# Cache attention, last sequence: the high parts of the output weights on GpSimd instead of ScalarE

## The chip, the cores and the metric

The kernel runs on one core of a Trainium2 chip. The metric is the device time of one execution in microseconds (us), the median of several runs. A profiled execution also has a span, from the first to the last instruction that the trace shows.

The core's engines run beside each other, each through its own list of instructions in order, and wait for each other by semaphores: TensorE (PE in the rows, PEld for its weight loads), VectorE (DVE), ScalarE (ACT), GpSimd (POOL) and SyncE (SP), which here issues most DMAs.

## The reference

One layer of a decoder runs for a prompt of 1024 tokens and for 8 decode tokens, each of which attends to its own 8192 cached positions. What matters here is the decode attention, in which a key is an up-projected latent beside a rotary part, normalised together, and the output projection that follows it:

```python
def update(carry, ckv_blk, kpe_blk, mask):
    m, l, acc = carry
    k = mla_keys(ckv_blk, kpe_blk, w_uk, g_kn).astype(jnp.float32)
    s = jnp.einsum('bqhd,bkhd->bhqk', qf, k) * scale
    ...
mixed = jnp.concatenate([rms_norm(pool_out, g_out[:POOL_WIDTH]),
                         rms_norm(attn_out, g_out[POOL_WIDTH:])], axis=-1)
x = x + mixed @ lp['w_o']
```

The gains `g_out` belong to rows of `w_o`, so the kernel multiplies them into the weights. All is 32-bit. A matmul operand is held as a high part, rounded to the type that TensorE takes in one pass (`fp32r` in the rows), and a low part, the rest; a product is then three matmuls: high by high, high by low, low by high.

## The kernel before, in words

The work goes through stages: inputs and heads, prompt attention, the cache stage with the output projection (`cache_and_merge`), gate and up projection, down projection. The change lies in the cache stage, in the last of its 8 sequences.

**The loop.** A sequence's 8192 positions are 64 tiles of 128, taken in 32 pairs; the loop variable is `n` (on GpSimd also `u`). Every engine has its own loop over the same pairs, written out by hand, and the order in each list is the order of the work:

- TensorE: `turn` (L1734) transposes the latents of pair n + 1 into `TT`; `keys` (L1760) waits for the residual `lo` of pair n (`lo_done`) and makes the keys of its two tiles, six matmuls each (L1768). At n = 18 `weigh` (L1772) sums the latents of the sequence before, weighted by the probabilities.
- ScalarE: `hi` (L1919) rounds the transposed latents; `squares` (L2011) squares the keys of pair n - 1 (L2016) and copies their scores (L2017), tile by tile.
- VectorE: `lo` (L2101) is the residual; `sums` (L2216) adds the squares of pair n - 1, first tile (L2220); then work of single values of n; then `rotary_scores` (L2223) reduces GpSimd's product of pair n - 2 (L2225); then `sums` for the second tile; at every fourth n `rotary_sums` (L2228).
- GpSimd: `product` (L1626, instruction at L1634) multiplies the rotary keys of pair n by the query, into one of two buffers. It waits until VectorE has reduced the product of pair n - 2 (`product_read`).

**The score tail.** When a sequence is through, GpSimd turns raw scores into normalised ones: `tail_mean` (L1639), `tail_raw` (L1650), `tail_norm` (L1658, a Newton step of four instructions, L119 to L122), `tail_scale` (L1664). Most instructions wait for the one before by a semaphore (`step`). In the last sequence three quarters of this (48 tiles, 384 numbers in a partition) are done inside the loop, after the products of n = 25, 26, 28 and 29; the rest follows the loop.

**The output weights.** While the last sequence runs, `w_o` (8 blocks of 128 rows, two halves of 512 columns, j = 0 to 15) is loaded and split. SyncE loads half j into one of two buffers `w_raw` when the low part of half j - 2 is made (L1567). ScalarE multiplies by the gain column and rounds: the high part `w_o_hi` (`split_w_o`, L1943, instruction at L1949). VectorE makes the low part `w_o_lo` (`split_w_o`, L2131, instruction at L2135). Halves 0 to 11 are made in the loop, one at each n of

```python
HALF_AT = tuple(n for n in range(19, PAIRS) if n != 28)
```

on ScalarE after the squares, on VectorE between the two `sums`, ahead of `rotary_scores`. At n = 28 VectorE makes the residual of the first mixed tile instead (L2143), of which ScalarE makes the square and the high part at n = 25 and 26. Halves 12 to 15 follow the loop. Then `project` (L1814) multiplies the mixed rows of 9 tiles by the weights.

Of the kernel before, what the change touches and what calls it, by code (L numbers as in the profile page):

```python
# [12 lines left out]
ALU = mybir.AluOpType  # L13
# [8 lines left out]
NB = 8  # L22
# [1354 lines left out]
HALF_AT = tuple(n for n in range(19, PAIRS) if n != 28)  # L1377
# [23 lines left out]
def cache_and_merge(nc, io, keep):  # L1401

    START, PACE = 36, 7
    with ExitStack() as stack:
# [97 lines left out]
        dve_step = c.sem("dve_step")  # L1502

        w_o_in = [c.sem(f"w_o_in{n}") for n in range(2)]
        w_o_hi_done, w_o_lo_done = c.sem("w_o_hi_done"), c.sem("w_o_lo_done")
        m_in = [c.sem(f"m_in{n}") for n in range(3)]
        x_in = [c.sem(f"x_in{n}") for n in range(XS)]
        stored = [c.sem(f"stored{n}") for n in range(XS)]
# [103 lines left out]
        @block.gpsimd  # L1612
        def _(pool):
            def chunk_sums(i):

                n = width(i)
                pool.wait_ge(mix_squared, i + 1)
                step(nc.gpsimd.tensor_tensor(msq[:, :, 0:2, 0:n], msq[:, :, 0:2, 0:n], msq[:, :, 2:4, 0:n], ALU.add))
                nc.gpsimd.tensor_tensor(msq[:, :, 0, 0:n], msq[:, :, 0, 0:n], msq[:, :, 1, 0:n], ALU.add)\
                  .then_inc(chunks_added, 1)  # L1620

            step = Steps(pool, pool_step)

            def product(b, u):

                par, k, made = b % 2, 2 * (u % 4), b * PAIRS + u  # L1626
                if u == 0:
                    pool.wait_ge(q_in[par], 16 * (b // 2 + 1))
                if u % 4 == 0:
                    pool.wait_ge(slot_in[par * CHUNKS + u // 4], 32 * (b // 2 + 1))  # L1630
                if made >= 2:
                    pool.wait_ge(product_read, made - 1)
                keys = kpe[:, (b * CHUNKS + u // 4) % RING, k * DR:(k + 2) * DR].rearrange("p (k d) -> p k d", d=DR)
                nc.gpsimd.tensor_tensor(products[u % 2][:].rearrange("p (k h) d -> p k h d", h=NH),  # L1634
                                        keys.unsqueeze(2).to_broadcast([P, 2, NH, DR]),
                                        q_row[par].rearrange("p (h d) -> p h d", d=DR).unsqueeze(1)
                                        .to_broadcast([P, 2, NH, DR]), ALU.mult).then_inc(product_made, 1)

            def tail_mean(b, a=0, z=TILES):  # L1639

                mean = ss[:, b % 2, a:z]
                if b >= 1 and a == 0:
                    pool.wait_ge(shifted, b)
                pool.wait_ge(summed, b * TILES + z)
                pool.wait_ge(pe_summed, b * CHUNKS + z // 8)
                step(nc.gpsimd.tensor_tensor(mean, mean, kss[:, b % 2, a:z].unsqueeze(2)
                                             .to_broadcast([P, z - a, NH]), ALU.add))
                nc.gpsimd.tensor_scalar(mean, mean, 1.0 / DH, EPS, ALU.mult, ALU.add).then_inc(averaged, 1)

            def tail_raw(b, a=0, z=TILES):  # L1650

                pool.wait_ge(scored, b * TILES + z)
                step(nc.gpsimd.tensor_tensor(raw[:, b % 2, a:z], raw[:, b % 2, a:z],
                                             keep.coef[:, b, :].unsqueeze(1).to_broadcast([P, z - a, NH]), ALU.mult))
                pool.wait_ge(product_read, b * PAIRS + z // 2)
                step(nc.gpsimd.tensor_tensor(raw[:, b % 2, a:z], raw[:, b % 2, a:z], rot[:, b % 2, a:z], ALU.add))

            def tail_norm(b, part=0, a=0, z=TILES):  # L1658

                pool.wait_ge(averaged, b + 1 + part)  # L1660
                pool.wait_ge(guessed, b + 1 + part)
                step(newton_rsqrt(nc.gpsimd, step, guess[:, a:z], ss[:, b % 2, a:z], guess[:, a:z], tmp[:, a:z]))

            def tail_scale(b, a=0, z=TILES):  # L1664
                step(nc.gpsimd.tensor_tensor(raw[:, b % 2, a:z], raw[:, b % 2, a:z], guess[:, a:z], ALU.mult))

            def tail_own(b):
                nc.gpsimd.tensor_copy(raw[:, b % 2, TILES, :], keep.s_new[:, b, :]).then_inc(complete, 1)

            def tail_shift(b):  # L1670
                pool.wait_ge(reduced, b + 1)
                nc.gpsimd.tensor_tensor(raw[:, b % 2], raw[:, b % 2], top_all[:].unsqueeze(1)
                                        .to_broadcast([P, TILES + 1, NH]), ALU.subtract).then_inc(shifted, 1)

            def paced(b, n):
                pool.wait_ge(summed, (b - 1) * TILES + START + PACE * n // 2)
                gather(nc, io, keep, b, (n,))

            def sequence(par, b, r):
                for n in range(PAIRS):  # L1680
                    if b == 0 and n % 4 == 0 and 4 <= n < 4 * (CHUNKS - 2):
                        pool.wait_ge(summed, 2 * n)
                        gather(nc, io, keep, 0, (n // 4 + 2,))
                    product(b, n)
                    if b >= 1:
                        if n == MEAN_AT:
                            tail_mean(b - 1)
                        if n == RAW_AT:
                            tail_raw(b - 1)
                        if n == NORM_AT:  # L1690
                            tail_norm(b - 1)
                        if n == OWN_AT:
                            tail_scale(b - 1)
                            tail_own(b - 1)
                        if n == SHIFT_AT:
                            tail_shift(b - 1)
                    if b + 1 < NB and n in GATHER_AT:
                        if GATHER_AT[n][0] == 0:
                            if b == 0:
                                pool.wait_ge(keep.mixed_stored, 16 * (1 + NH // 2))  # L1700
                            else:
                                pool.wait_ge(weighted, b)
                        for k in GATHER_AT[n]:
                            paced(b + 1, k)
                    if b == NB - 1 and n == 25:
                        tail_mean(b, *PARTS[0])
                    if b == NB - 1 and n == 26:
                        tail_raw(b, *PARTS[0])
                    if b == NB - 1 and n == 28:
                        tail_norm(b, 0, *PARTS[0])  # L1710
                    if b == NB - 1 and n == 29:
                        tail_scale(b, *PARTS[0])

            gather(nc, io, keep, 0, (1, 2))
            sequences(pool, sequence)
            chunk_sums(0)
            b = NB - 1
            tail_mean(b, *PARTS[1])
            tail_raw(b, *PARTS[1])
            tail_norm(b, 1, *PARTS[1])  # L1720
            tail_scale(b, *PARTS[1])
            tail_own(b)
            chunk_sums(1)
            tail_shift(b)
            for i in range(2, NT):
                chunk_sums(i)
            down.gpsimd(pool)
# [184 lines left out]
        def _(act):  # L1912
            def sequence(par, b, r):
                later = b > 0
                for n in range(PAIRS):
# [16 lines left out]
                        square_rotary(par, b, n // 4)  # L1932
                    if b < NB - 1 and n in HI_AT:
                        split_w(b + 1, HI_AT.index(n))
                    if b == NB - 1:
                        if n in HALF_AT:
                            split_w_o(HALF_AT.index(n))
                        if n == 25:
                            square_mixed(0)
                        if n == 26:  # L1940
                            split_mixed(0)

            def split_w_o(j):  # L1943

                k, g = divmod(j, 2)
                act.wait_ge(w_o_in[g], 16 * (k + 1))
                if j == 0:
                    act.wait_ge(weighted, NB - 1)
                nc.scalar.activation(w_o_hi[:, k, g * 512:(g + 1) * 512], w_raw[g][:], ACT.Copy,  # L1949
                                     scale=keep.g_out[:, k:k + 1]).then_inc(w_o_hi_done, 1)  # L1950

            def square_mixed(i):

# [115 lines left out]
        def _(dve):  # L2069
# [61 lines left out]
            def split_w_o(j):  # L2131

                k, g = divmod(j, 2)
                dve.wait_ge(w_o_hi_done, j + 1)
                nc.vector.scalar_tensor_tensor(out=w_o_lo[:, k, g * 512:(g + 1) * 512], in0=w_raw[g][:],  # L2135
                                               scalar=keep.g_out[:, k:k + 1],
                                               in1=w_o_hi[:, k, g * 512:(g + 1) * 512].bitcast(F32), op0=ALU.mult,
                                               op1=ALU.subtract).then_inc(w_o_lo_done, 1)
# [736 lines left out]
```

## Time and profile before

| | us |
|---|---|
| median of 3 runs | 2211.56 |
| the runs | 2207.08, 2211.56, 2211.88 |
| the profiled execution | 2210.82 |
| its span | 2209.0 |
| TensorE busy | 2155.2 |
| VectorE busy | 1530.3 |
| ScalarE busy | 972.2 |
| GpSimd busy | 702.2 |

How to read it: "busy" adds up the instructions of an engine, whether or not something waits for them. The loop over the cache runs from about 415 to 1303 us of the span, the last of its 8 sequences at the end; the granted TensorE clock is full in all slices of the page. A row of the timeline gives start, duration, engine, line, operation, what is written from what, shapes, and in brackets how long the engine had been idle before and who released it.

### The profile page before, as it was taken

The page shows a single profiled execution, that of the slowest core. Times are in us where ns is not written, and L with a number is a line of the kernel's source. Part 1 is how long each engine was busy: PE and PEld are TensorE (multiplying, and loading weights), DVE is VectorE, ACT ScalarE, POOL GpSimd, SP SyncE. Part 2 cuts the span into 40 slices and gives each one's busy share as a digit, 9 for nine tenths or more (in the row PEclk, how much of TensorE's full clock was granted, in tenths as well). Part 3 has the DMA queues.
Part 4 walks back from the last instruction along what each step waited for, and adds up shares of the span by engine and source line. Part 5 has one row for each costly group of instructions (what it writes and reads, how often), then busy time and mean ns, then how long its engine had stood idle before and what let it go on. Part 6 is the DMA issues. An engine that isn't in the chain of part 4 may idle for free.

```text
span 2209.0 us, 33857 instructions
## 1 busy us (share of the span) xinstructions
PE 2155.2 (98%) x12537; PEld 1801.5 (82%) x12537; DVE 1530.3 (69%) x2353; ACT 972.2 (44%) x2273; POOL 702.2 (32%) x765
## 2 busy tenths in 40 slices
PE   8998899999999999999999989999999999999999
PEld 7987566788787878787878767799999999977776
DVE  4447676688787878787878785666767677654345
ACT  4445566556565656565656553312111111233333
POOL 1554211367474747474747352100000000000000
PEclk9999999999999999999999999999999999999999
DMA  5210100243131313131314032221111111044353
GB/s 163 66 29 1 61 16 20 84 141 124 66 115 59 121 53 128 48 132 46 134 43 149 25 129 96 78 75 44 47 47 47 47 47 44 23 174 148 132 188 125
DMA packets 95811, 183.20 MB, mean 83 GB/s; under 512 B 9416, under 2 KB 65568, under 8 KB 87311
## 3 DMA queue, kind: packets, MB, share of 16 engines
q1 hardware_dynamic: 79933, 96.53, 13.3%
q0 software_dynamic: 15744, 84.93, 11.3%
q8 instruction: 79, 1.29, 0.2%
q14 instruction: 55, 0.45, 0.1%
HBM read 167.39 MB, written 14.36 MB: 82 GB/s over the span
## 4 chain that ended last, share of the span: by engine, by line
PE 77%; DVE 3%; ACT 0%; issue 0%; DMA 0%; POOL 0%; SPq 0%; ACTq 0%; DVEq 0%; POOLq 0%
PE ca_banks L1768 31%; PE ca_banks L2376 22%; PE ca_banks L2649 11%; PE ca_banks L1744 5%; PE ca_banks L1828 4%; PE ca_banks L1780 3%; PE ca_banks L2625 0%; DVE ca_cells L2225 0%; DVE ca_cells L2220 0%; DVE ca_lo L2101 0%; PE ca_banks L1859 0%; DVE ca_room L2487 0%; DVE ca_down_lo L2689 0%; DMA ca_x<-in_x_prompt 0%; ACT ca_down_hi L2680 0%
## 5 line engine op out<-in xcount | busy, mean ns | idle before, releaser
L2016 ACT ACTIVATE ca_banks<-ca_banks 128x512 f32<-128x512 f32 x512 | 298.2, 582 | 324.1 <-PE ca_banks L1768 319.6
L1768 PE MATMUL ca_banks<-cache_w_hi,ca_hi 128*128 128x512 f32 x1024 | 427.6, 418 | 6.5 <-DVE ca_lo L2101 5.6
L2220 DVE TENSOR_REDUCE ca_cells<-ca_banks 128x8 f32<-128x512 f32 x512 | 352.3, 688 | 87.9 <-ACT ca_banks L2016 72.7
L1768 PE MATMUL ca_banks<-cache_w_lo,ca_hi 128*128 128x512 f32 x1024 | 403.0, 394 | 0.0
L1768 PE MATMUL ca_banks<-cache_w_hi,ca_lo 128*128 128x512 f32 x1024 | 401.3, 392 | 0.0
L1768 PEld LDWEIGHTS ca_banks<-cache_w_hi,ca_lo 128*128 128x128 f32 x1024 | 193.1, 189 | 46.5
L1768 PEld LDWEIGHTS ca_banks<-cache_w_hi,ca_hi 128*128 128x128 f32 x1024 | 192.9, 188 | 44.7 <-DVE ca_lo L2101 10.4
L1768 PEld LDWEIGHTS ca_banks<-cache_w_lo,ca_hi 128*128 128x128 f32 x1024 | 193.6, 189 | 32.3
L1634 POOL TENSOR_TENSOR ca_product<-cache_kpe,attn_q_row_odd 128x512 f32<-128x512 f32 x128 | 164.7, 1290 | 171.4 <-DVE ca_cells L2225 169.9
L2101 DVE TENSOR_TENSOR ca_lo<-ca_banks,ca_hi 128x512 fp32r<-128x512 f32 x256 | 175.0, 684 | 56.7 <-ACT ca_hi L1919 56.2
L1634 POOL TENSOR_TENSOR ca_product<-cache_kpe,ca_q_row_even 128x512 f32<-128x512 f32 x128 | 164.7, 1293 | 130.6 <-DVE ca_cells L2225 129.3
L1919 ACT ACTIVATE ca_hi<-ca_banks 128x512 fp32r<-128x512 f32 x256 | 154.5, 604 | 55.7 <-PE ca_banks L1744 55.7
L2225 DVE TENSOR_REDUCE ca_cells<-ca_product 128x16 f32<-128x512 f32 x256 | 172.9, 676 | 2.9 <-POOL ca_product L1634 2.9
L2572 POOL DMA_DIRECT2D out_new_conv_prompt<-ca_y x1 | 0.6, 612 | 542.3 <-ACT ca_y L2663 542.3
L2487 DVE RECIPROCAL ca_room<-ca_room 128x1032 f32<-128x1032 f32 x22 | 145.3, 6603 | 0.8
L2689 DVE TENSOR_TENSOR ca_down_lo<-ca_down_raw,ca_down_hi 128x1024 fp32r<-128x1024 f32 x44 | 53.9, 1225 | 97.0 <-ACT ca_down_hi L2680 97.0
L2421 ACT ACTIVATE ca_room<-ca_banks 128x1032 f32<-128x1032 f32 x22 | 22.8, 1036 | 219.9 <-PE ca_banks L2376 219.9
L2649 PE MATMUL ca_banks<-ca_down_hi,ca_g_hi 128*128 128x512 f32 x352 | 113.9, 405 | 2.2 <-DVE ca_gT L2490 1.9
L2376 PE MATMUL ca_banks<-mlp_h_hi,ca_gate_hi 128*128 128x344 f32 x528 | 113.4, 321 | 0.6 <-DVE mlp_h_lo L2185 0.6
L2376 PE MATMUL ca_banks<-mlp_h_lo,ca_gate_hi 128*128 128x344 f32 x528 | 113.3, 320 | 0.0
L2376 PE MATMUL ca_banks<-mlp_h_hi,ca_gate_lo 128*128 128x344 f32 x528 | 112.7, 319 | 0.0
L2376 PE MATMUL ca_banks<-mlp_h_hi,ca_up_hi 128*128 128x344 f32 x528 | 112.2, 321 | 0.0
(400 smaller groups left out, 4323.3 us busy)
## 6 DMA issues: line engine op xcount, KB each, us to landing
ca_down_raw<-in_w_down SPq DMA_DIRECT2D x44, 512.0 KB, 3.3
keep_w_uv<-in_w_gate SPq DMA_DIRECT2D x22, 512.0 KB, 3.8
ca_up_raw<-in_w_up SPq DMA_DIRECT2D x22, 512.0 KB, 3.6
keep_ctx<-in_w_down SPq DMA_DIRECT2D x22, 512.0 KB, 3.7
late_room<-in_x_prompt SPq DMA_DIRECT2D x8, 512.0 KB, 3.6
ca_m<-mixed_scratch SPq DMA_DIRECT2D x8, 512.0 KB, 5.3
ca_w_raw<-in_w_o SPq DMA_DIRECT2D x16, 256.0 KB, 2.5
ca_x<-in_x_prompt SPq DMA_DIRECT2D x8, 512.0 KB
```

Source lines behind the costliest of these rows:

```text
L1634: nc.gpsimd.tensor_tensor(products[u % 2][:].rearrange("p (k h) d -> p k h d", h=NH), keys.unsqueeze(2).to_broadcast([P, 2, NH, DR]), q_ro ...
L1744: last = nc.tensor.transpose(TT[:, n % 2, (2 * t + ck) * P:(2 * t + ck + 1) * P], src, keep.ident[:])
L1768: last = nc.tensor.matmul(KK[:, t, :], x[:, n % 2, t, ck, :], w[:, par, ck, :], start=(m == 0), stop=(m == 5))
L1828: last = nc.tensor.matmul(OUT[0:n, a, g, :], h[:, k, 0:n], w[:, k, g * 512:(g + 1) * 512], start=(k == 4 * a and q == 0), stop=(k == 4 * a ...
L1919: nc.scalar.activation(hi[:, n % 2], TT[:, n % 2, :].rearrange("p (t c k) -> p t c k", t=2, c=2), ACT.Copy).then_inc(hi_done, 1)
L2016: nc.scalar.activation(SQ[:, t, :], KK[:, t, :], ACT.Square).then_inc(squared, 1)
L2101: nc.vector.tensor_tensor(lo[:, n % 2], TT[:, n % 2, :].rearrange("p (t c k) -> p t c k", t=2, c=2), hi[:, n % 2].bitcast(F32), ALU.subtra ...
L2220: nc.vector.tensor_reduce(ss[:, par, 2 * n + t, :], SQ[:, t, :].rearrange("p (h d) -> p h d", d=DN), AX.X, ALU.add).then_inc(summed, 1)
L2225: nc.vector.tensor_reduce(rot[:, par, 2 * u:2 * u + 2, :].rearrange("p t h -> p (t h)"), products[u % 2][:], AX.X, ALU.add).then_inc(produ ...
L2376: ins = nc.tensor.matmul(GU[kind][:, j, :], w[kind][:, k, :], h[:, k, j * F3:(j + 1) * F3], start=(k == 0 and n == 0), stop=(k == DC - 1 a ...
L2487: link(nc.vector.reciprocal(sig, sig))
L2649: last = nc.tensor.matmul(self.OUT[t][:, h, :], g[b][:, t * P:(t + 1) * P], w[b][:, h * 512:(h + 1) * 512], start=(f == 0 and k == 0), sto ...
```

## The change

GpSimd gets a function `raise_w_o`, called in the last sequence at each n of `HALF_AT`, ahead of `product(b, n)`. It makes the high part of halves 0 to 11 by one `tensor_scalar` with the gain column; at the first it also waits for `weighted`, as ScalarE did. ScalarE's `split_w_o` is no longer called in the loop; it makes halves 12 to 15 after it, as before, and counts them by a semaphore of their own. VectorE waits for the one count or the other.

```diff
-        w_o_hi_done, w_o_lo_done = c.sem("w_o_hi_done"), c.sem("w_o_lo_done")
+        w_o_hi_done, w_o_hi_rest, w_o_lo_done = c.sem("w_o_hi_done"), c.sem("w_o_hi_rest"), c.sem("w_o_lo_done")
...
+            def raise_w_o(j):
+
+                k, g = divmod(j, 2)
+                pool.wait_ge(w_o_in[g], 16 * (k + 1))
+                if j == 0:
+                    pool.wait_ge(weighted, NB - 1)
+                nc.gpsimd.tensor_scalar(w_o_hi[:, k, g * 512:(g + 1) * 512], w_raw[g][:], keep.g_out[:, k:k + 1], None,
+                                        ALU.mult).then_inc(w_o_hi_done, 1)
...
+                    if b == NB - 1 and n in HALF_AT:
+                        raise_w_o(HALF_AT.index(n))
                     product(b, n)
...
-                    if b == NB - 1:
-                        if n in HALF_AT:
-                            split_w_o(HALF_AT.index(n))
-                        if n == 25:
-                            square_mixed(0)
-                        if n == 26:
-                            split_mixed(0)
+                    if b == NB - 1 and n == 25:
+                        square_mixed(0)
+                    if b == NB - 1 and n == 26:
+                        split_mixed(0)
...
                 act.wait_ge(w_o_in[g], 16 * (k + 1))
-                if j == 0:
-                    act.wait_ge(weighted, NB - 1)
                 nc.scalar.activation(w_o_hi[:, k, g * 512:(g + 1) * 512], w_raw[g][:], ACT.Copy,
-                                     scale=keep.g_out[:, k:k + 1]).then_inc(w_o_hi_done, 1)
+                                     scale=keep.g_out[:, k:k + 1]).then_inc(w_o_hi_rest, 1)
...
-                dve.wait_ge(w_o_hi_done, j + 1)
+                dve.wait_ge(w_o_hi_done, min(j + 1, len(HALF_AT)))
+                if j >= len(HALF_AT):
+                    dve.wait_ge(w_o_hi_rest, j + 1 - len(HALF_AT))
```

## Rows read from the trace of the kernel before

**Rows 1.** The page, busy time, share of the span and instructions of each engine.
```profile
PE 2155.2 (98%) x12537; PEld 1801.5 (82%) x12537; DVE 1530.3 (69%) x2353; ACT 972.2 (44%) x2273; POOL 702.2 (32%) x765
```
**Rows 2.** The chain that ended last, in order of time: start, duration, work.
```profile
1213.32 2.78 PE ca_banks L1768 x12
1216.54 2.78 PE ca_banks L1768 x12
...
1245.62 7.44 PE ca_banks L1780 x130
...
1281.90 3.06 PE ca_banks L1768 x12
...
1300.69 3.03 PE ca_banks L1768 x12
```
**Rows 3.** The timeline, slots 25 and 26 of the last sequence.
```profile
1278.00 0.58 ACT L2016 ACTIVATE ca_banks<-ca_banks 128x512 f32<-128x512 f32 x1 [0.69 <-PE ca_banks L1768]
...
1278.55 0.72 ACT L1949 ACTIVATE ca_w_o_hi<-ca_w_raw,keep_g_out 128x512 fp32r<-128x512 f32 x1
...
1279.31 0.75 DVE L2135 SCALAR_TENSOR_TENSOR ca_w_o_lo<-ca_w_raw,keep_g_out,ca_w_o_hi 128x512 fp32r<-128x512 f32 x1 [0.50 <-ACT ca_w_o_hi L1949]
...
1279.98 0.68 DVE L2225 TENSOR_REDUCE ca_cells<-ca_product 128x16 f32<-128x512 f32 x1
...
1280.57 0.68 DVE L2220 TENSOR_REDUCE ca_cells<-ca_banks 128x8 f32<-128x512 f32 x1
...
1280.73 1.27 POOL L1634 TENSOR_TENSOR ca_product<-cache_kpe,attn_q_row_odd 128x512 f32<-128x512 f32 x1 [2.28 <-DVE ca_cells L2225]
...
1281.17 0.68 DVE L2101 TENSOR_TENSOR ca_lo<-ca_banks,ca_hi 128x512 fp32r<-128x512 f32 x1
...
1281.90 0.50 PE L1768 MATMUL ca_banks<-cache_w_hi,ca_hi 128*128 128x512 f32 x1 [0.18 <-DVE ca_lo L2101]
```
**Rows 4.** Line L1949, ScalarE's high parts: durations (ns min/median/max), who waited for them.
```profile
L1949 ACT ACTIVATE ca_w_o_hi<-ca_w_raw,keep_g_out x16: 722/724/726, 1257.0 to 1311.1; 128x512 fp32r<-128x512 f32 x16
...
  DVE ca_w_o_lo L2135: 8.0, 14
```
**Rows 5.** The timeline again, slots 19, 27, 28, 30 and 31.
```profile
1257.76 0.75 DVE L2135 SCALAR_TENSOR_TENSOR ca_w_o_lo<-ca_w_raw,keep_g_out,ca_w_o_hi 128x512 fp32r<-128x512 f32 x1 [1.39 <-ACT ca_w_o_hi L1949]
...
1286.31 0.75 DVE L2135 SCALAR_TENSOR_TENSOR ca_w_o_lo<-ca_w_raw,keep_g_out,ca_w_o_hi 128x512 fp32r<-128x512 f32 x1 [0.51 <-ACT ca_w_o_hi L1949]
...
1290.83 0.68 DVE L2225 TENSOR_REDUCE ca_cells<-ca_product 128x16 f32<-128x512 f32 x1
...
1291.65 1.28 POOL L1634 TENSOR_TENSOR ca_product<-cache_kpe,attn_q_row_odd 128x512 f32<-128x512 f32 x1 [2.36 <-DVE ca_cells L2225]
...
1297.00 1.29 POOL L1634 TENSOR_TENSOR ca_product<-cache_kpe,attn_q_row_odd 128x512 f32<-128x512 f32 x1
1297.12 1.73 DVE L2135 SCALAR_TENSOR_TENSOR ca_w_o_lo<-ca_w_raw,keep_g_out,ca_w_o_hi 128x512 fp32r<-128x512 f32 x1 [0.37 <-ACT ca_w_o_hi L1949]
...
1301.45 0.75 DVE L2135 SCALAR_TENSOR_TENSOR ca_w_o_lo<-ca_w_raw,keep_g_out,ca_w_o_hi 128x512 fp32r<-128x512 f32 x1 [0.21 <-ACT ca_w_o_hi L1949]
```
**Rows 6.** Groups of GpSimd by line and shape: busy us, mean ns, idle before.
```profile
L1634 POOL TENSOR_TENSOR ca_product<-cache_kpe,attn_q_row_odd 128x512 f32<-128x512 f32 x128 | 164.7, 1290 | 171.4 <-DVE ca_cells L2225 169.9
...
L121 POOL TENSOR_SCALAR keep_w_uv<-keep_w_uv 128x512 f32<-128x512 f32 x7 | 4.3, 620 | 0.6
...
L1653 POOL TENSOR_TENSOR ca_cells<-ca_cells,attn_coef 128x384 f32<-128x384 f32 x1 | 1.0, 1015 | 0.0
...
L1646 POOL TENSOR_TENSOR ca_cells<-ca_cells 128x384 f32<-128x384 f32 x1 | 0.9, 862 | 0.0
...
L121 POOL TENSOR_SCALAR keep_w_uv<-keep_w_uv 128x384 f32<-128x384 f32 x1 | 0.5, 512 | 0.1
...
L1130 POOL TENSOR_SCALAR keep_ctx<-keep_ctx 8x8 f32<-8x8 f32 x1 | 0.2, 239 | 0.1
...
L1134 POOL TENSOR_SCALAR keep_ctx<-keep_ctx 8x8 f32<-8x8 f32 x1 | 0.2, 186 | 0.1
```

## Prediction

> **What bounds the kernel now.** I read the page first, then the chain of waits, then the timeline of the stretch that the diff touches. The page says that TensorE is busy for nearly the whole span, while ScalarE and GpSimd have room [rows 1]; by that alone, work moved between these two costs nothing. The averages hide the stretch that matters. In the chain, a pair of cache tiles (one turn n of the loop, below "slot n") normally follows the one before after 1216.54 - 1213.32 = 3.22 us: TensorE's own twelve products and four transposes [rows 2]. In slots 19 to 31 of the last sequence the pace is slower: from slot 26 (1281.90) to slot 31 (1300.69) there are five slots in 18.79 us, 3.76 each, and the row at 1281.90 is released by VectorE, not by TensorE's own queue [rows 2, 3]. So this stretch, some 45 us long, is bound by a ring of other engines, and the change rebuilds that ring.
>
> **The ring now** [rows 3]. ScalarE squares the second tile (1278.00), then makes the high half (1278.55 to 1279.27); VectorE, idle for 0.50, starts the low half at 1279.31, then the rotary reduction 0.67 later, then one sum, then the residual `ca_lo` at 1281.17, and TensorE starts at 1281.90. The high half, 0.72 each, delayed VectorE by 8.0 us in 14 of the 16 halves [rows 4]. GpSimd is not in the ring: its product starts at 1280.73, just after the reduction that frees its buffer, and is needed two slots later.
>
> **Taken away.** Twelve ScalarE instructions, 12 x 0.72 = 8.7 us busy, and with them VectorE's waits. Worth at most: the whole stretch back at TensorE's pace. The low halves of slots 19 and 31 start at 1257.76 and 1301.45, 43.69 us apart [rows 5]; twelve slots at 3.22 are 38.64, so 5.0 us is the ceiling of the gain.
>
> **Put in: a wait, and what queues behind it.** GpSimd runs in order. In slot n it now does the high half, then `product(n)`, then (slots 25, 26, 28, 29) pieces of the score tail. `product(n)` waits for rotary reduction n-2, which VectorE does in slot n *behind* its low half, and the low half waits for GpSimd's high half, which stands behind `product(n-1)`. That closes a new ring of one slot: low half, reduction, product, next high half, next low half. Its length from rows:
> - low half to reduction 1279.98 - 1279.31 = 0.67; reduction 0.68; hand-over to GpSimd 0.07 (1280.66 to 1280.73) in one slot and 0.14 (1291.51 to 1291.65) in another, mean 0.10 [rows 3, 5];
> - product 1.29 [rows 6]; high half on GpSimd, r, unknown; hand-over to VectorE about 0.05 (1279.27 to 1279.31 from ScalarE) [rows 3].
>
> Together 2.79, taken as 2.80 + r, per slot.
>
> **The price r.** No row has GpSimd scale by a per-partition column into this type, so I bound it. Below: a GpSimd tensor_scalar of the same 128x512 with constants, 0.62. Above: the two-input form, 1.29 [rows 6]. One input, one output and the same element count put it next to 0.62; I add 0.05, the difference of the one-operation and the two-operation form at 8x8 (0.239 and 0.186) [rows 6], since this one has one operation: **r = 0.67**. The ring is then 3.47 a slot: above TensorE's 3.22, below the 3.64 of today (43.69 / 12). Plain slots get slightly faster.
>
> The Trainium skill (GPSIMD Engine Reference, section 4.1 Engine selection) sends elementwise work to VectorE, calling GpSimd about 2x slower with two inputs and near line rate with one. By the 2x and VectorE's 0.75 low half r would be 1.5 and the change 15 us slower, an estimate; the one-input row of this trace, 0.62, sides with the page's second half.
>
> **The tail pieces.** Today they delay only a product that nobody needs for two slots. Now each stands between a product and the next high half, so in the ring in full. With 0.86 and 1.02 for the two kinds of 128x384 two-input operation, 0.51 for the one-input one, and 0.09 (0.6 / 7) after each for its step wait [rows 6]: mean, slot 25, 0.86 + 0.09 + 0.51 = 1.46; raw, slot 26, 2 x 1.11 = 2.22; scale, slot 29, 1.11: together 4.79. Slot 28 has no half: from the low half of slot 27 (1286.31) VectorE runs without a wait to the reduction of slot 28 (1290.83), 4.52 [rows 5]; plus 0.68, 0.10 and 1.29 is 6.59; the norm piece, four operations, is 0.86 + 1.02 + 0.51 + 1.02 + 4 x 0.09 = 3.77; then r and 0.05. From slot 27 to slot 29 that is 10.41 + r.
>
> **The sum.** In slot 19 VectorE was ready 1.39 before it started: 1257.76 - 1.39 = 1256.37 [rows 5]. GpSimd's first half waits only for the weighted sum, over at 1245.62 + 7.44 = 1253.06 [rows 2], so it is in time. From there ten plain slots (19 to 27, 29 to 31), the three tail pieces and the double slot: 10 x (2.80 + r) + 4.79 + 10.41 + r = 43.20 + 11r. The low half of slot 31 starts at 1299.57 + 11r = 1306.94, against 1301.45: **5.5 us later**. The residual that TensorE waits for stands behind the low half on VectorE, so TensorE is late by the same. With r = 0.62 the loss is 4.9, with r = 1.29 it is 12.3; the change breaks even only at r = 0.17.
>
> **The rest costs nothing.** The loads of the next halves on SyncE wait for low halves two back; a ring of over 3.4 us a slot leaves over 6 us for them. The four last halves stay on ScalarE, and they, the remaining loads, GpSimd's last tail quarter and the projection all follow slot 31, so they shift with it; nothing later waits for something that isn't shifted. ScalarE's lighter queue gives nothing more, since the ring no longer passes it.
>
> **The shared port.** In slot 30 a low half took 1.73 instead of 0.75, started while a GpSimd product (1297.00, 1.29 long) was running [rows 5]. The new ring keeps low halves and GpSimd apart, since each waits for the other, so I charge nothing.
> The Trainium skill (SBUF — State Buffer, Who interferes with whom) says that a VectorE instruction with two SBUF inputs and a GpSimd one that reads SBUF block each other for a whole instruction; the 1.73 agrees, and the sum would be the same by it.
>
> **Rivals.**
> *A. The new ring does not bind, and the change is faster.* One mechanism: GpSimd runs the half while VectorE is busy with sums and residual, and every slot returns to 3.22. It decides below r = 3.22 - 2.80 = 0.42, with the tail pieces hidden besides. Gain 5.0: 2205.8. Against it: the cheapest row is 0.62 [rows 6], and the order in the code leaves no place to hide a tail piece. Chance 0.04.
> *B. An even swap.* Today's pace is already 3.64, the new ring 3.47; if GpSimd's hand-overs and step gaps are shorter than I charge, or the tail pieces partly hide, little is left of the loss. With all three pieces of slots 25, 26 and 29 free it is 5.5 - 4.8 = +0.7, 2211.5; halfway, 2214. For it: the forecast lies near the line. Against it: each piece is in program order ahead of a half that VectorE awaits. Chance 0.24, and 0.02 that ScalarE stays in the ring by another way (its squares and copies), with no change to see.
> *C. GpSimd pays the two-input price*, for the column operand or the rounding to the matmul type: r up to 1.29, +12.3, 2223.1. The Trainium skill (GPSIMD Engine Reference, section 4.1) points this way only for two inputs. For it: no row of the exact form. Against it: the one-input rows. Chance 0.18.
>
> **The numbers.** Forecast, chance 0.52: the profiled execution took 2210.82 (span 2209.0), 0.7 below the median of the runs, 2211.56. 2210.82 + 5.5 = 2216.3; its own range, r from 0.62 to 0.85, is 2215.7 to 2218.3. The range over cases goes from B's end, 2211.0, to C's, 2223.2. About 0.2%, 4.4 us, is what a measurement of this kernel can tell from no change: slower by more is the forecast and C, 0.70; within is B, 0.26; faster is A, 0.04.
>
> **What would show it.** Right: GpSimd's new line at 0.62 to 0.85 a half; VectorE's idle time before the low halves released by GpSimd, about 0.4 in plain slots and 1.5 to 4 us in slots 26, 27, 29 and 30; GpSimd's idle time before its products still ended by the reduction; low halves about 3.47 apart in slots 19 to 25; slot 31's low half some 50.6 us after slot 19's readiness. Wrong: TensorE at 3.22 a slot there (A), low halves over 4 us apart in plain slots (C), or no long wait in slots 26, 27, 29 and 30 (B).

## The result and the profile after

The changed kernel took 2226.46 us in the median of 6 runs against 2208.01 for the kernel before in runs beside them: a ratio of 1.0076, 95% interval 1.0061 to 1.0090, or 13.5 to 19.9 us slower. The direction was forecast; the size, 5.5 us within 2211.0 to 2223.2, was not.

The profiled execution took 2221.05, the shortest of the six, and entered the stretch of the change 2.9 us earlier than the one before did. So the traces are compared over that stretch alone, from the start of the weighted sum in slot 18 (first product of that line) to the first product with the output weights. The first fence is the busy time in the stretch before (start and end, length, then busy us and instructions of TensorE, its weight loads, VectorE, ScalarE and GpSimd, the granted clock, the DMA share, GB/s), the second the same after.

```profile
1245.62:1304.41 58.79, 54.63 (x350) 40.32 (x351) 46.02 (x75) 36.59 (x91) 27.50 (x24) 1.00 0.16 54
```
```profile
1242.69:1315.91 73.22, 58.80 (x351) 43.16 (x351) 45.00 (x75) 29.78 (x79) 44.25 (x36) 0.93 0.13 44
```

The stretch is 73.22 - 58.79 = 14.4 us longer: this is where the time went. After it the two traces take the same to within 1.2 us (2209.0 - 1304.41 = 904.6 and 2219.3 - 1315.91 = 903.4). ScalarE is 6.8 us lighter; GpSimd is 16.8 us heavier. On the page of the changed kernel (busy time, then the chain that ended last) the averages hardly move [rows 1], but GpSimd has entered the chain:

```profile
PE 2157.3 (97%) x12537; PEld 1800.9 (81%) x12537; DVE 1528.7 (69%) x2353; ACT 964.7 (43%) x2261; POOL 719.1 (32%) x777
...
PE 76%; DVE 2%; POOL 2%; issue 1%; DMA 0%; ACT 0%; SPq 0%; POOLq 0%; DVEq 0%; ACTq 0%
```

The chain of waits of the changed kernel, in order of time, shows the new ring turn by turn; one turn, slot 20 to 21 (start, duration, work):

```profile
1259.15 1.28 POOL ca_product L1634
1260.43 1.56 POOL ca_w_o_hi L1645
1261.99 0.03 issue
1262.02 0.04 DVE ca_w_o_lo L2143
1262.05 0.63 issue
1262.68 0.69 DVE ca_cells L2233
1263.37 0.07 issue
1263.45 1.27 POOL ca_product L1634
```

Product, high half, low half (its successor starts 0.67 after it), reduction, product: 4.30 us, and TensorE, whose 3.22 filled the chain before [rows 2], is not in it. The groups of GpSimd's new line (shapes, count, busy us, mean ns) and the waits in the stretch (who waited for whom: us, times, longest):

```profile
L1645 POOL TENSOR_SCALAR ca_w_o_hi<-ca_w_raw,keep_g_out 128x512 fp32r<-128x512 f32 x12 | 18.8, 1567 | 5.9 <-PE ca_banks L1791 5.5
```
```profile
DVE ca_w_o_lo L2143 <- POOL ca_w_o_hi L1645: 20.2, 11, 4.9
...
PE ca_banks L1779 <- DVE ca_lo L2107: 12.8, 8, 4.6
```

A high half takes 1.57 us on GpSimd, not 0.67, and VectorE waits 20.2 us for GpSimd. In the kernel before it waited 4.7 us for ScalarE in the stretch; the 8.0 us of [rows 4] count the four halves behind the loop too.

```profile
DVE ca_w_o_lo L2135 <- ACT ca_w_o_hi L1949: 4.7, 12, 1.4
```

The timeline has the low halves of slots 19, 23 to 27 and 29 to 31 (the tail pieces come in at 26, 27, 29 and 30), and TensorE behind that of slot 29:

```profile
1253.36 0.74 DVE L2143 SCALAR_TENSOR_TENSOR ca_w_o_lo<-ca_w_raw,keep_g_out,ca_w_o_hi 128x512 fp32r<-128x512 f32 x1
...
1270.56 0.75 DVE L2143 SCALAR_TENSOR_TENSOR ca_w_o_lo<-ca_w_raw,keep_g_out,ca_w_o_hi 128x512 fp32r<-128x512 f32 x1 [1.12 <-POOL ca_w_o_hi L1645]
...
1274.84 0.75 DVE L2143 SCALAR_TENSOR_TENSOR ca_w_o_lo<-ca_w_raw,keep_g_out,ca_w_o_hi 128x512 fp32r<-128x512 f32 x1 [0.81 <-POOL ca_w_o_hi L1645]
...
1279.18 0.75 DVE L2143 SCALAR_TENSOR_TENSOR ca_w_o_lo<-ca_w_raw,keep_g_out,ca_w_o_hi 128x512 fp32r<-128x512 f32 x1 [1.20 <-POOL ca_w_o_hi L1645]
...
1284.99 0.75 DVE L2143 SCALAR_TENSOR_TENSOR ca_w_o_lo<-ca_w_raw,keep_g_out,ca_w_o_hi 128x512 fp32r<-128x512 f32 x1 [2.67 <-POOL ca_w_o_hi L1645]
...
1291.43 0.75 DVE L2143 SCALAR_TENSOR_TENSOR ca_w_o_lo<-ca_w_raw,keep_g_out,ca_w_o_hi 128x512 fp32r<-128x512 f32 x1 [3.30 <-POOL ca_w_o_hi L1645]
...
1303.31 0.75 DVE L2143 SCALAR_TENSOR_TENSOR ca_w_o_lo<-ca_w_raw,keep_g_out,ca_w_o_hi 128x512 fp32r<-128x512 f32 x1 [4.89 <-POOL ca_w_o_hi L1645]
...
1305.90 0.79 PE L1779 MATMUL ca_banks<-cache_w_hi,ca_hi 128*128 128x512 f32 x1 [4.57 <-DVE ca_lo L2107]
...
1308.66 0.75 DVE L2143 SCALAR_TENSOR_TENSOR ca_w_o_lo<-ca_w_raw,keep_g_out,ca_w_o_hi 128x512 fp32r<-128x512 f32 x1 [2.21 <-POOL ca_w_o_hi L1645]
...
1312.94 0.75 DVE L2143 SCALAR_TENSOR_TENSOR ca_w_o_lo<-ca_w_raw,keep_g_out,ca_w_o_hi 128x512 fp32r<-128x512 f32 x1 [1.14 <-POOL ca_w_o_hi L1645]
```

### The profile page after: what moved, and what is told of

It is laid out like the page before. It is cut to its first block, busy times and chain, and to the rows that moved or that the text cites. A ratio compares the mean times of both kernels' runs of the same rounds, so it can differ in the third digit from the quotient of the medians.

```text
span 2219.3 us, 33861 instructions
## 1 busy us (share of the span) xinstructions
PE 2157.3 (97%) x12537; PEld 1800.9 (81%) x12537; DVE 1528.7 (69%) x2353; ACT 964.7 (43%) x2261; POOL 719.1 (32%) x777
## 3 DMA queue, kind: packets, MB, share of 16 engines
q8 instruction: 79, 1.29, 0.2%
## 4 chain that ended last, share of the span: by engine, by line
PE 76%; DVE 2%; POOL 2%; issue 1%; DMA 0%; ACT 0%; SPq 0%; POOLq 0%; DVEq 0%; ACTq 0%
PE ca_banks L1779 30%; PE ca_banks L2384 22%; PE ca_banks L2657 11%; PE ca_banks L1755 5%; PE ca_banks L1839 4%; PE ca_banks L1791 3%; POOL ca_w_o_hi L1645 1%; POOL ca_product L1634 1%; DVE ca_cells L2233 1%; PE ca_banks L2633 0%; DVE ca_cells L2228 0%; PE ca_banks L1870 0%; DVE ca_room L2495 0%; DMA ca_x<-in_x_prompt 0%; DVE ca_lo L2107 0%
## 5 line engine op out<-in xcount | busy, mean ns | idle before, releaser
L1779 PEld LDWEIGHTS ca_banks<-cache_w_hi,ca_hi 128*128 128x128 f32 x1024 | 194.1, 190 | 54.4 <-DVE ca_lo L2107 20.2
```

Source lines behind the costliest of these rows:

```text
L1779: last = nc.tensor.matmul(KK[:, t, :], x[:, n % 2, t, ck, :], w[:, par, ck, :], start=(m == 0), stop=(m == 5))
```

## The experiments

All are edits of the changed kernel. The two kernels that mix forms were run once, for their rows. "Stretch" is the one above: 58.79 us in the kernel before, 73.22 in the changed one, each read from the one trace of its kernel. A ratio is to the kernel before in runs beside that experiment, with its 95% interval. Two questions: why is the high half so dear, and is its place in the ring the whole loss?

**Six forms in one kernel.** Each half takes one of six forms in turn.

```diff
-                nc.gpsimd.tensor_scalar(w_o_hi[:, k, g * 512:(g + 1) * 512], w_raw[g][:], keep.g_out[:, k:k + 1], None,
-                                        ALU.mult).then_inc(w_o_hi_done, 1)
+                hi, raw, col, form = w_o_hi[:, k, g * 512:(g + 1) * 512], w_raw[g][:], keep.g_out[:, k:k + 1], j % 6
+                if form == 0:
+                    made = nc.gpsimd.tensor_scalar(hi, raw, col, None, ALU.mult)
+                elif form == 1:
+                    made = nc.gpsimd.tensor_scalar(hi, raw, col, 1.0, ALU.mult, ALU.mult)
+                elif form == 2:
+                    made = nc.gpsimd.tensor_scalar(hi, raw, 1.0, None, ALU.mult)
+                elif form == 3:
+                    made = nc.gpsimd.tensor_scalar(hi, raw, 1.0, 1.0, ALU.mult, ALU.mult)
+                elif form == 4:
+                    made = nc.gpsimd.tensor_tensor(hi, raw, col.to_broadcast([P, 512]), ALU.mult)
+                else:
+                    made = nc.gpsimd.tensor_copy(hi, raw)
+                made.then_inc(w_o_hi_done, 1)
```

> The twelve halves on GpSimd are made by six forms in turn (j modulo 6): column and no second operation, column and a second operation by 1.0, constant 1.0 and no second operation, two constants, a two-input product with the column broadcast, and a plain copy. Where a constant or a copy stands, the gain is left out of the high part (the low part, made from the gained weights less the high part, takes it up). Theory 'one operation is the slow form': halves without a second operation take about 1.56, with one about 0.62 to 0.7, whether column or constant. Rival 'the column operand': 1.56 wherever the column stands as an operand (forms 0 and 1), 0.62 for constants. Rival 'rounding to the matmul type': all of them at 1.3 or more. In each, if the ring of one slot sets the pace, the low halves are 2.72 plus that half's price apart (4.28 measured less 1.56); if something else sets it, the distance does not follow the price.

GpSimd's groups by line, in the order of forms 0, 2, 4, 1, 3, 5:

```profile
L1647 POOL TENSOR_SCALAR ca_w_o_hi<-ca_w_raw,keep_g_out 128x512 fp32r<-128x512 f32 x2 | 3.1, 1570 | 5.5 <-PE ca_banks L1803 5.5
...
L1651 POOL TENSOR_SCALAR ca_w_o_hi<-ca_w_raw 128x512 fp32r<-128x512 f32 x2 | 3.0, 1490 | 0.1
...
L1655 POOL TENSOR_TENSOR ca_w_o_hi<-ca_w_raw,keep_g_out 128x512 fp32r<-128x512 f32 x2 | 2.1, 1042 | 0.1
...
L1649 POOL TENSOR_SCALAR ca_w_o_hi<-ca_w_raw,keep_g_out 128x512 fp32r<-128x512 f32 x2 | 1.4, 696 | 0.1
...
L1653 POOL TENSOR_SCALAR ca_w_o_hi<-ca_w_raw 128x512 fp32r<-128x512 f32 x2 | 1.2, 620 | 0.1
...
L1657 POOL CAST ca_w_o_hi<-ca_w_raw 128x512 fp32r<-128x512 f32 x2 | 1.2, 610 | 0.0
```

Both rivals fall: the column adds 0.08, the rounding type nothing (a copy into it takes 0.61). The missing second operation costs 0.87: 1.57 against 0.70 with the column, 1.49 against 0.62 with the constant. Even the two-input product is faster, 1.04. The ring follows the price. VectorE's low halves in the timeline, slots 21 to 25, the last four behind forms 3, 4, 5 and 0:

```profile
1265.21 0.75 DVE L2155 SCALAR_TENSOR_TENSOR ca_w_o_lo<-ca_w_raw,keep_g_out,ca_w_o_hi 128x512 fp32r<-128x512 f32 x1 [0.81 <-POOL ca_w_o_hi L1651]
...
1268.55 0.75 DVE L2155 SCALAR_TENSOR_TENSOR ca_w_o_lo<-ca_w_raw,keep_g_out,ca_w_o_hi 128x512 fp32r<-128x512 f32 x1 [0.19 <-POOL ca_w_o_hi L1653]
...
1272.30 0.75 DVE L2155 SCALAR_TENSOR_TENSOR ca_w_o_lo<-ca_w_raw,keep_g_out,ca_w_o_hi 128x512 fp32r<-128x512 f32 x1 [0.61 <-POOL ca_w_o_hi L1655]
...
1275.68 0.74 DVE L2155 SCALAR_TENSOR_TENSOR ca_w_o_lo<-ca_w_raw,keep_g_out,ca_w_o_hi 128x512 fp32r<-128x512 f32 x1
...
1280.04 0.75 DVE L2155 SCALAR_TENSOR_TENSOR ca_w_o_lo<-ca_w_raw,keep_g_out,ca_w_o_hi 128x512 fp32r<-128x512 f32 x1 [1.23 <-POOL ca_w_o_hi L1647]
```

They are 3.34, 3.75, 3.38 and 4.36 apart; 2.72 plus the price is 3.34, 3.76, 3.33 and 4.29.

**A cost per element or per instruction.** Halves in pieces of 256 and 128 columns, and whole with an addition of 0.0 as the second operation.

```diff
-                nc.gpsimd.tensor_scalar(w_o_hi[:, k, g * 512:(g + 1) * 512], w_raw[g][:], keep.g_out[:, k:k + 1], None,
-                                        ALU.mult).then_inc(w_o_hi_done, 1)
+                hi, raw, col, form = w_o_hi[:, k, g * 512:(g + 1) * 512], w_raw[g], keep.g_out[:, k:k + 1], j % 4
+                if form == 0:
+                    for a in (0, 256):
+                        made = nc.gpsimd.tensor_scalar(hi[:, a:a + 256], raw[:, a:a + 256], col, None, ALU.mult)
+                elif form == 1:
+                    for a in (0, 128, 256, 384):
+                        made = nc.gpsimd.tensor_scalar(hi[:, a:a + 128], raw[:, a:a + 128], col, None, ALU.mult)
+                elif form == 2:
+                    for a in (0, 256):
+                        made = nc.gpsimd.tensor_scalar(hi[:, a:a + 256], raw[:, a:a + 256], col, 1.0, ALU.mult, ALU.mult)
+                else:
+                    made = nc.gpsimd.tensor_scalar(hi, raw[:], col, 0.0, ALU.mult, ALU.add)
+                made.then_inc(w_o_hi_done, 1)
```

> The twelve halves in four forms in turn (j modulo 4): one operation in two pieces of 256 columns, one operation in four pieces of 128, two operations in two pieces of 256, and two operations with the second an addition of 0.0. Theory 'a cost per element': 256 columns with one operation about 0.85 (half of 1.57 and a little), 128 about 0.47, the pieces together somewhat over 1.57; 256 with two operations about 0.42. Rival 'a fixed cost of the form': each piece carries the 0.87 that 512 columns showed, so 256 columns about 1.3 and 128 about 1.15. The addition of 0.0 as the second operation about 0.70, if it is the number of operations that counts and not their kind.

GpSimd's groups, forms 1, 0, 2, 3:

```profile
L1651 POOL TENSOR_SCALAR ca_w_o_hi<-ca_w_raw,keep_g_out 128x128 fp32r<-128x128 f32 x12 | 7.0, 604 | 0.1
L1648 POOL TENSOR_SCALAR ca_w_o_hi<-ca_w_raw,keep_g_out 128x256 fp32r<-128x256 f32 x6 | 5.5, 925 | 5.6 <-PE ca_banks L1802 5.5
L1654 POOL TENSOR_SCALAR ca_w_o_hi<-ca_w_raw,keep_g_out 128x256 fp32r<-128x256 f32 x6 | 2.8, 477 | 0.1
L1656 POOL TENSOR_SCALAR ca_w_o_hi<-ca_w_raw,keep_g_out 128x512 fp32r<-128x512 f32 x3 | 2.1, 692 | 0.1
```

One operation: 0.604, 0.925 and 1.567 for 128, 256 and 512 columns, (1567 - 604) / 384 = 2.5 ns per element over about 0.28 us of start. Two operations: 0.477 and 0.692, 0.84 ns per element over 0.26. So the extra cost is per element; the start, which the theory left out, makes the pieces dearer than it put them (0.925 against 0.85, 0.604 against 0.47). Adding 0.0 as the second operation costs the same as multiplying by 1.0.

**Two operations throughout.**

```diff
-                nc.gpsimd.tensor_scalar(w_o_hi[:, k, g * 512:(g + 1) * 512], w_raw[g][:], keep.g_out[:, k:k + 1], None,
-                                        ALU.mult).then_inc(w_o_hi_done, 1)
+                nc.gpsimd.tensor_scalar(w_o_hi[:, k, g * 512:(g + 1) * 512], w_raw[g][:], keep.g_out[:, k:k + 1], 1.0,
+                                        ALU.mult, ALU.mult).then_inc(w_o_hi_done, 1)
```

> The high halves keep the column and get a second multiplication by 1.0. Theory 'one operation is the slow form': each half about 0.65, low halves 3.35 to 3.4 apart in plain slots, about 10 us less than the changed kernel, still about 0.2% above the kernel before (ratio 1.001 to 1.003). Rivals (column operand, rounding): still about 1.56 a half and a ratio of about 1.007.

Ratio 1.0025 (1.0011 to 1.0038), some 5.5 us above the kernel before. GpSimd's group, and busy time in the stretch:

```profile
L1645 POOL TENSOR_SCALAR ca_w_o_hi<-ca_w_raw,keep_g_out 128x512 fp32r<-128x512 f32 x12 | 8.3, 694 | 5.9 <-PE ca_banks L1791 5.5
```
```profile
1240.66:1304.44 63.78, 53.79 (x351) 40.19 (x351) 44.91 (x75) 29.43 (x79) 33.94 (x36) 1.00 0.15 50
```

The stretch is 9.4 us shorter than in the changed kernel by this alone and 5.0 longer than before. The ring of plain slots is 3.42 to 3.50.

**Halves ahead of the tail pieces.** With the slow form, then with two operations.

```diff
-                    if b == NB - 1 and n in HALF_AT:
-                        raise_w_o(HALF_AT.index(n))
+                    if b == NB - 1 and n == HALF_AT[0]:
+                        raise_w_o(0)
                     product(b, n)
+                    if b == NB - 1 and n + 1 in HALF_AT[1:]:
+                        raise_w_o(HALF_AT.index(n + 1))
```

> The high half for slot n + 1 stands right behind the product of slot n, ahead of the tail pieces, which were 8.6 us of the ring. Theory 'each tail piece stood in the ring in full': mean and scale now hide behind the wait for the reduction, raw shows 0.7 and norm 2.3, so about 5.5 us less than the changed kernel (ratio to the kernel before about 1.005); the plain slots stay at 4.28. Rival 'the pieces were hidden already': no change against the changed kernel (ratio 1.0076).

Ratio 1.0067 (1.0046 to 1.0087), whose interval overlaps the changed kernel's, so the runs do not tell the two apart; the trace does:

```profile
1245.84:1315.23 69.39, 56.37 (x350) 41.43 (x351) 47.51 (x74) 28.92 (x77) 45.18 (x36) 0.98 0.15 46
```

The stretch is 3.8 us shorter than the changed kernel's, instead of 5.5. The pieces did stand in the ring, but taken out of it they run beside low halves. One of four such, and the GpSimd instruction that was running:

```profile
1291.39 1.02 POOL L1662 TENSOR_TENSOR ca_cells<-ca_cells,attn_coef 128x384 f32<-128x384 f32 x1
...
1291.46 1.50 DVE L2145 SCALAR_TENSOR_TENSOR ca_w_o_lo<-ca_w_raw,keep_g_out,ca_w_o_hi 128x512 fp32r<-128x512 f32 x1 [1.13 <-POOL ca_w_o_hi L1645]
```

1.50 instead of 0.75; the four (1.33, 1.50, 1.31, 1.47) add 2.6 us. That is more than the 1.7 that are missing, so it is enough to explain them; what each of the four costs the ring is not shown.

> Two operations in a half, and the half of slot n + 1 ahead of the tail pieces of slot n. With two operations alone the stretch from the weighted sum to the projection was 5.0 us longer than in the kernel before; putting the halves ahead of the tail pieces gave 3.8 us back with the slow form (5.5 less what low halves of 1.3 to 1.5 took). Theory: plain slots at 3.42, the stretch 1.2 us longer than before, ratio about 1.0005. Rival: with the shorter half the pieces no longer fit behind the wait for the reduction and nothing is given back, ratio about 1.0025.

Ratio 1.0008 (0.9997 to 1.0018), no change that the runs can tell; the rival's 1.0025 lies outside. The stretch is 1.7 us over the kernel before, against 1.2 expected:

```profile
1241.66:1302.13 60.47, 55.20 (x350) 41.44 (x351) 47.44 (x74) 28.69 (x76) 35.41 (x36) 0.97 0.17 53
```

**Halves one slot early.** With the slow form, then with two operations.

```diff
-                    if b == NB - 1 and n in HALF_AT:
-                        raise_w_o(HALF_AT.index(n))
+                    if b == NB - 1 and n + 1 in HALF_AT:
+                        raise_w_o(HALF_AT.index(n + 1))
                     product(b, n)
```

> GpSimd makes each high half one slot earlier, ahead of the product before, so that a low half no longer waits for the product between. Theory 'the order on GpSimd alone made the ring': the stretch returns to TensorE's 3.22 a slot, about 5 us less than the kernel before (ratio about 0.998). Rival 'the shared port comes in': low halves now start while GpSimd runs, and either engine stands still for the other's instruction; low halves of 1.5 to 2.3 instead of 0.75 and a time between the two kernels or above the changed one.

Ratio 1.0017 (1.0002 to 1.0031). The stretch, the low halves of slots 19 and 26, and that of slot 30:

```profile
1240.27:1300.76 60.49, 54.36 (x351) 40.91 (x351) 48.80 (x74) 28.84 (x77) 48.90 (x36) 0.97 0.15 53
```
```profile
1250.95 0.99 DVE L2143 SCALAR_TENSOR_TENSOR ca_w_o_lo<-ca_w_raw,keep_g_out,ca_w_o_hi 128x512 fp32r<-128x512 f32 x1
...
1274.00 0.92 DVE L2143 SCALAR_TENSOR_TENSOR ca_w_o_lo<-ca_w_raw,keep_g_out,ca_w_o_hi 128x512 fp32r<-128x512 f32 x1
...
1292.50 1.73 DVE L2143 SCALAR_TENSOR_TENSOR ca_w_o_lo<-ca_w_raw,keep_g_out,ca_w_o_hi 128x512 fp32r<-128x512 f32 x1 [2.79 <-POOL ca_w_o_hi L1645]
```

Both theories hold in part, and the time is the rival's. Up to slot 26 the low halves are (1274.00 - 1250.95) / 7 = 3.29 apart: the ring is gone although the half is as dear as ever. But the engines now overlap: halves on GpSimd take up to 2.54 instead of 1.56, and low halves up to 1.77, like the last row. And in slots 27, 30 and 31 VectorE still waits for GpSimd, 3.6 us in all.

> Two operations in a half, and each half a slot early. With the slow form this order ran at 3.29 a slot up to slot 26 and lost time where GpSimd was late after the tail pieces; the stretch was 1.7 us longer than before. Theory 'GpSimd was late by its load alone': 0.87 less a half frees it, the stretch is 1.5 to 5 us shorter than in the kernel before, ratio 0.9977 to 0.9993. Rival 'the shared port sets the loss': low halves of 1.3 to 1.8 in slots 26 to 31 remain, ratio 1.000 to 1.002.

Ratio 0.9984 (0.9974 to 0.9994), as the theory had it and outside the rival's range: this version is about 0.16% faster than the kernel before. Busy time in its stretch, and the low half of slot 30:

```profile
1248.52:1304.84 56.32, 53.15 (x351) 40.14 (x351) 46.87 (x75) 29.32 (x79) 36.55 (x36) 1.00 0.18 57
```
```profile
1297.42 1.77 DVE L2143 SCALAR_TENSOR_TENSOR ca_w_o_lo<-ca_w_raw,keep_g_out,ca_w_o_hi 128x512 fp32r<-128x512 f32 x1 [1.01 <-POOL ca_w_o_hi L1645]
```

2.5 us less than before, half of the 5.0 that the prediction set as the ceiling. In slots 27 to 31 the low halves still take 1.46, 1.04, 1.77 and 1.12, and that of slot 30 waits 1.01 for GpSimd, which is late after the norm piece. That these make up the other half is likely, but not shown: freeing those slots of the tail pieces was not tried.

## Why the prediction was wrong

- *The bound and the ring now* held: the stretch was bound by the ring of ScalarE and VectorE. With the halves off ScalarE and one slot early, the low halves of slots 19 to 26 came 3.29 apart; in the kernel before, those of slots 19 to 27 were (1286.31 - 1257.76) / 8 = 3.57 apart [rows 5]. After the stretch nothing changed beyond 1.2 us.
- *The new ring* held, step by step. Without the price, a turn was put at 2.80 and measured 4.28 - 1.56 = 2.72 (low halves of slots 23 and 24 at 1270.56 and 1274.84). The tail pieces, put at 1.46, 2.22 and 1.11, added 1.53, 2.16 and 1.07 to the turns of 26, 27 and 30 (5.81, 6.44 and 5.35, less 4.28). Slots 27 to 29: 10.41 + r put, 1303.31 - 1291.43 = 11.88 measured, that is 10.32 and 1.56.
- *The price r* is the step that failed: "r = 0.67", bounded by 0.62 and 1.29. It was 1.57. With it the sum, 43.20 + 11r, gives 60.5 from slot 19 to 31; the trace has 1312.94 - 1253.36 = 59.6. With r = 0.69 forced by a second operation, the forecast's 5.5 us came out: 5.0 in the stretch, 5.5 by the ratio. So of the stretch's 14.4 us, 9.4 are the price and 5.0 the ring that was forecast.
- Why r was read wrong: the row that showed the one-operation form was 8 elements long [rows 6], 0.053 slower, and was added as a fixed cost. At 2.5 - 0.84 = 1.66 ns per element, 8 elements show 0.013 of it and 512 show 0.85. And the upper end was no bound: the two-input row, 1.29, was taken to be dearer than any one-input form; a two-input product is cheaper (1.04 to 1.29) than the one-operation form at 1.57.
- Rival C had the effect (low halves over 4 us apart) but neither its cause, column or rounding, nor its size: the loss lies above its +12.3 as r lies above 1.29. Rival A was excluded for this order, as measured, but half of its gain was there with two operations and the half one slot early. Rival B's tail pieces did not hide.
- The Trainium skill (GPSIMD Engine Reference, section 4.1 Engine selection) puts one-input operations near line rate. Here the two-operation form (0.62 to 0.70) and the copy (0.61) fit, beside VectorE's 0.75 for a low half; the one-operation form, 1.57, does not. That the estimate of 15 us from its 2x came near the stretch's 14.4 is luck: it is a rule for two inputs.
- *The shared port* was rightly charged at nothing for this order: all low halves in the ring take 0.75. Every order tried that lets GpSimd work beside low halves pays it. The Trainium skill (SBUF — State Buffer, Who interferes with whom) says that a VectorE instruction with two SBUF inputs contends with a GpSimd one that reads SBUF; the 1.50 and 1.73 above agree.
- *The rest* held. The last 2.4 us between the stretch's 14.4 and the ratio's middle, 16.8, lie within the interval.

## What to carry to other kernels

When work moves to an engine with room, draw the ring that its place in that engine's order closes, and sum one turn: here it gave the loss in the stretch to within a microsecond once the price was right. The price of an instruction must come from a row of the same form and of similar length; a neighbouring form is no bound, even where it does more work, as the two-operation and the two-input rows did here; and a short row tells a start-up cost, not a rate. On GpSimd give `tensor_scalar` a second operation (times 1.0): 0.69 us instead of 1.57 for 512 elements.

## What was not expected of the hardware

GpSimd's `tensor_scalar` takes 2.5 ns per element with one operation and 0.84 with two, with a column as the operand; with a constant, 512 elements cost 1.49 and 0.62. And TensorE's granted clock fell twice in the changed kernel's stretch, while in the kernel before it stayed full there. It was 0.50 (1.2 GHz) in 1288 to 1290, after a wait of 2.31 us for the residual of slot 27, and from 1306 to 1310, after the wait of 4.57 for that of slot 30; a product took 0.63 instead of 0.39 in the timeline. The first fence is the first product of slot 27, the second has windows of 2 us:

```profile
1287.58 0.80 PE L1779 MATMUL ca_banks<-cache_w_hi,ca_hi 128*128 128x512 f32 x1 [2.31 <-DVE ca_lo L2107]
```
```profile
1288.00:1290.00 2.00, 2.00 (x6) 1.52 (x6) 0.13 (x1) 1.11 (x3) 1.82 (x3) 0.50 0.00 0
...
1306.00:1308.00 2.00, 2.00 (x5) 1.61 (x6) 0.45 (x1) 0.50 (x2) 1.90 (x2) 0.50 0.02 6
1308.00:1310.00 2.00, 2.00 (x6) 1.52 (x6) 1.34 (x3) 0.67 (x2) 0.62 (x1) 0.50 0.00 0
```

The two falls together explain the 4.2 us more that TensorE is busy in the stretch (58.80 against 54.63): some 20 products at 0.24 more each. They cost no time in this trace, since every later low half was still released by GpSimd's high half. In the trace with two operations and the halves ahead of the tail pieces such a fall did cost: TensorE ran at 0.50 from 1300 to 1302 and went without a pause from its last key product into the projection, 3.53 us after the last low half of the loop instead of 2.96. That is about 0.6 of that trace's 1.7 us.
